# A two-layer decoder step on one core: the last additions of gathered rows partly on TensorE, and the samples' rows summed and normalized in four groups of partitions ahead of the last tile

## The chip, the core and the metric

One core of a Trainium2 chip runs the whole program. The metric is the time of one execution in device microseconds. Three runs of the kernel before gave 1462.3, 1465.44 and 1460.7 us, median 1462.3. The engines are TensorE (PE, and PEld for its weight loads), VectorE (DVE), ScalarE (ACT), GpSimd (POOL) and SyncE (SP); SP, ACT and POOL issue DMAs.

## What is computed

The reference runs a trunk of two layers over a prompt of 512 rows and over 8 sample rows, all 1024 wide. A layer is a mixer (attention and a gated recurrence in layer 0, causal mean pooling in layer 1) and then a mixture of 32 experts, of which each row uses two. The end of a layer and of the program, cut from the reference:

```python
    for layer in range(DEPTH):
        ...
        x = x + mix.astype(x.dtype)
        h = rmsnorm(x, norm_ffn[layer])
        x = x + hier_moe(h, ...)
    y = rmsnorm(x, norm_final)
```

`rmsnorm(x, g)` is `x * rsqrt(mean(x*x) + eps) * g` row by row, in float32 throughout.

## The kernel before

The 520 rows stand in SBUF as five tiles `x[:, t, :]`: tiles 0 to 3 have the prompt's 128 rows each, tile 4 (`NT`) has the 8 sample rows on 8 partitions. `TILES` is 5.

The experts of a layer are taken in 16 pairs (`PAIRS`), 64 gathered rows for each expert of a pair. SP streams three weight matrices for each pair into a ring of slots; in the first four pairs (`TURNS`) of a layer a fourth slot in the arena (`fourth`) takes part. PE computes gate products and up products (`products`), DVE and ACT make the activation, PE computes the results, and ACT scales them into `yst`. POOL gathers each pair's rows and scatters each pair's results but the last's into `y_rows` in HBM, through its own DMA queue. Each of the 520 rows has two places there, set 0 and set 1.

When the last pair has read its weights, `load_results` on SP brings `y_rows` back: one DMA for each tile into `gat[t]`, which has the two sets side by side and signals `x_in[t]`. The last pair's own results don't go through HBM. PE multiplies `memT`, a map of rows, with `yst`, in `rows_of_last(t)`, into the two PSUM banks from `LAST_BANK[t]` on, and signals `last_done`.

DVE then does, tile by tile, `combine(l, t)` (x plus set 0, and plus set 1 unless `ADDED_BY_PE[l]` lists it) and `add_last(l, t)` (x plus the two PSUM banks, signal `moe_added`). What `ADDED_BY_PE` lists is added by PE in the same PSUM group, by matmuls of the identity with the gathered rows: before the change that is set 1 of tile 3 and both sets of the samples, in layer 1 alone. For layer 0, `combine` and `add_last` feed the pooled mixer of layer 1: `pooled_rows` (DVE), `mix` (PE), `mixed_columns` (ACT), `maps` (PE), where the first `maps` waits until three tiles have had `add_last`.

At the end of the program each tile goes through ACT's `mean_root` (a Square with a sum along the row at L919, a root at L920), DVE's `normed_rows` (a reciprocal at L1270 and a product with root and gain at L1271), and a store that ACT issues at L1250. All queues are in the order of the program text. DVE's loop is `combine(u)`, `add_last(u)`, then the normalization of tile `u - 1`; ACT's loop is the root of tile `u`, then the store of tile `u - 1`. The samples are the last tile in every queue. Lines in the trace: L732 the gathers of `load_results`, L1202 and L1210 ACT's two instructions of a pair, L1570 and L1573 the sets in `combine`, L1583 `add_last`, L2202 `mix`, L1153 `mixed_columns`, L2223 `maps`, L2238 and L2252 or L2276 the products and results of experts, L2437 the transposes of the next pair's rows, L2503 the gathered sets on PE and L2504 the last pair's rows, L845 POOL's gather.

Of the kernel before, what the change touches and what calls it, by code (L numbers as in the profile page):

```python
# [75 lines left out]
def shape_constants():  # L76
# [44 lines left out]
    for g, w in enumerate(WINDOWS):  # L121
        for b in range(NB):
# [4 lines left out]
            (("c_zero", np.zeros((1, ZEROS))), ("c_onehot", onehot), ("c_square", square), ("c_small", small), ("c_masks", masks), ("c_pool", pools))}  # L127


def build(nc, a, outs, consts):  # L130
# [11 lines left out]
    with ExitStack() as ctx:  # L142
# [93 lines left out]
        ADDED_BY_PE = ((), ((NT - 1, 1), (NT, 0), (NT, 1)))  # L236
# [78 lines left out]
        ecmp = at(26900, NOV, NE)  # L315
        fourth = [at(lo, PIECE) for lo in (0, 22216)]
# [73 lines left out]
        QUERIES, LOGITS, PROBS_TURNED, ATTENDED, GATES_TURNED, HEADS_TURNED = range(1, 7)  # L390
# [3 lines left out]
        LB_EXPED, SAMPLE_ROOT, DECODE_EXPED, HEAD_ROOTS, GATES_OUT, LATE_OUT = range(1, 7)  # L394
# [236 lines left out]
        def _(sp):  # L631
# [93 lines left out]
            def load_results(l):  # L725
# [86 lines left out]
        def _(pool):  # L812
# [43 lines left out]
            for l in range(2):  # L856
# [11 lines left out]
                for i in range(PAIRS):  # L868
# [7 lines left out]
                    if l == 0 and i == TURNS - 1:  # L876
# [7 lines left out]
                        for g in range(NG):  # L884
                            pool.dma_start(poolw[:, g], a["pool_w"][0, g].rearrange("(k p) c -> p k c", p=P)).then_inc(pool_in, 16)
                pool.wait_ge(y_stored, 16 * (PAIRS - 1) * (l + 1))
# [23 lines left out]
        def _(act):  # L910
# [330 lines left out]

            for u in range(TILES + 1):
                if u < TILES:
                    act.wait_ge(moe_added, TILES + u + 1)
                    mean_root(4, u, x[0:rows_of(u), u, :], spare)
                t = u - 1
                if t >= 0:
                    act.wait_ge(y_final, t + 1)
                    dst = y_prompt.rearrange("b (t p) d -> p (b t) d", p=P)[:, t, :] if t < NT else y_sample.rearrange("b t d -> (b t) d")
                    act.dma_start(dst, x[0:rows_of(t), t, :]).then_inc(stored, 16)  # L1250

            act.wait_ge(stored, 16 * (1 + TILES))
# [8 lines left out]
        def _(dve):  # L1261
# [314 lines left out]
            def add_last(l, t):  # L1576
# [5 lines left out]
                dve.wait_ge(last_done, TILES * l + t + 1)  # L1582
# [27 lines left out]
            def experts(l):  # L1610
# [97 lines left out]
                else:  # L1708
# [154 lines left out]
            for u in range(TILES + 1):  # L1863
                if u < TILES:
                    if u < NT:
                        combine(1, u)
                    add_last(1, u)
# [718 lines left out]
```

## Time and profile before

| | us |
|---|---|
| median of the three runs | 1462.3 |
| profiled execution, whole | 1464.38 |
| its span, first to last instruction | 1462.6 |
| PE busy | 1270.1 (87%) |
| DVE busy | 358.3 (24%) |
| ACT busy | 247.4 (17%) |
| POOL busy | 83.6 (6%) |
| DMA over the span | 492.94 MB, 337 GB/s |
| mean granted TensorE clock | 0.948 |

Busy shares are means over stages with different limits. In the views of the trace times are in microseconds from the span's start. A line of the timeline gives start, duration, engine, line, operation, output and input with shapes, and a count; in brackets stands the engine's idle time before it and what ended that. A float32 matmul shows as two passes, two records each.

### The profile page before, as it was taken

How to read it: one execution, taken by the hardware profiler on the slowest of the kernel's cores; microseconds unless marked ns; L12 is line 12 of the kernel's file. 1: busy time of each engine (PE TensorE's matmuls, PEld its weight loads, DVE VectorE, ACT ScalarE, POOL GpSimd, SP SyncE). 2: the span in 40 equal slices, each digit the busy share in tenths (PEclk: the TensorE clock that was granted, in tenths of full speed). 3: DMA queues.
4: the chain of work that ended last, by engine and by line, in shares of the span. 5: the costliest groups of instructions: out<-in, count | busy, mean ns of one | idle time of the engine just before them, and what ended most of it. 6: DMA issues, size and time to landing. Idle time of an engine off the chain costs nothing.

```text
span 1462.6 us, 14567 instructions
## 1 busy us (share of the span) xinstructions
PE 1270.1 (87%) x5864; PEld 614.8 (42%) x5864; DVE 358.3 (24%) x826; ACT 247.4 (17%) x442; POOL 83.6 (6%) x101
## 2 busy tenths in 40 slices
PE   7999999999999877878878798999978777888886
PEld 3688965644543322223322235843333222232332
DVE  2065487522431000010100016551010000010006
ACT  3243643342110000000000003410000000000002
POOL 1000000000000100000000000000000000000000
PEclk9999999999999989999999999889999999999999
DMA  9435667327489999999999999369999999999995
GB/s 347 106 83 169 220 189 200 109 80 317 187 333 429 425 402 422 429 426 425 426 426 426 427 413 370 135 255 418 427 429 425 429 426 428 428 421 425 422 416 212
DMA packets 82446, 492.94 MB, mean 337 GB/s; under 512 B 17197, under 2 KB 21965, under 8 KB 59350
## 3 DMA queue, kind: packets, MB, share of 16 engines
q1 hardware_dynamic: 65968, 449.35, 75.5%
q0 software_dynamic: 13568, 37.03, 7.6%
q10 hardware_dynamic: 2862, 5.91, 1.1%
q8 instruction: 31, 0.51, 0.1%
q14 instruction: 17, 0.14, 0.0%
HBM read 479.75 MB, written 36.56 MB: 353 GB/s over the span
## 4 chain that ended last, share of the span: by engine, by line
PE 52%; DMA 37%; DVE 7%; issue 2%; ACT 2%; ACTq 0%; SPq 0%; DVEq 0%
DMA ring<-in_moe_w 35%; PE ps L2238 22%; PE ps L1912 5%; PE ps L1905 4%; PE ps L2164 3%; PE ps L2276 3%; PE ps L2350 1%; PE ps L2223 1%; PE ps L2263 1%; PE ps L2252 1%; PE ps L2304 1%; DVE arena L1366 1%; PE ps L2202 1%; PE ps L1954 1%; PE ps L2293 1%
## 5 line engine op out<-in xcount | busy, mean ns | idle before, releaser
L2238 PE MATMUL ps<-ring,arena 128*64 128x512 f32 x1920 | 470.0, 648 | 110.3 <-DMA ring<-in_moe_w 108.4
L2238 PEld LDWEIGHTS ps<-ring,arena 128*64 128x64 f32 x1920 | 146.8, 148 | 428.8 <-issue 279.4
L1781 DVE TENSOR_TENSOR arena<-arena,ps 128x512 f32<-128x512 f32 x32 | 22.0, 687 | 773.5 <-ACT arena L1202 773.5
L2276 PE MATMUL ps<-ring,arena 128*64 128x512 f32 x832 | 187.0, 602 | 26.3 <-issue 18.3
L2276 PEld LDWEIGHTS ps<-ring,arena 128*64 128x64 f32 x832 | 68.5, 138 | 126.9 <-issue 118.1
L1905 PE MATMUL ps<-arena,ring 128*128 128x260 f32 x512 | 115.7, 384 | 0.9 <-ACT arena L936 0.9
L1202 ACT ACTIVATE arena<-ps 128x512 f32<-128x512 f32 x32 | 19.1, 597 | 570.0 <-PE ps L2238 570.0
L1905 PEld LDWEIGHTS ps<-arena,ring 128*128 128x128 f32 x512 | 96.0, 190 | 17.0 <-issue 1.7
L1210 ACT ACTIVATE arena<-ps,arena 128x1024 f32<-128x1024 f32 x32 | 35.6, 1114 | 325.9 <-PE ps L2276 280.9
L1912 PE MATMUL ps<-ring,arena 128*128 128x512 f32 x192 | 86.0, 594 | 0.0
L845 POOL DMA_INDIRECT arena<-hn_rows,arena x30 | 30.6, 1021 | 528.7 <-PE ps L2437 477.0
L2164 PE MATMUL ps<-ring,arena 128*128 128x512 f32 x128 | 56.6, 595 | 0.0
L1912 PEld LDWEIGHTS ps<-ring,arena 128*128 128x128 f32 x192 | 35.3, 190 | 37.3 <-issue 36.8
L851 POOL DMA_INDIRECT y_rows<-arena x30 | 30.3, 1010 | 333.9 <-ACT arena L1210 333.9
L2437 PEld LDWEIGHTS ps<-arena 128*128 128x128 f32 x240 | 28.8, 191 | 26.5 <-issue 23.5
L1682 DVE TENSOR_TENSOR arena<-ps,arena 128x1024 f32<-128x1024 f32 x32 | 38.9, 1214 | 1.8 <-PE ps L2359 1.8
L2437 PE MATMUL ps<-arena 128*128 128x128 f32 x240 | 34.5, 287 | 2.1 <-DMA arena<-hn_rows,arena 2.1
L2462 PE MATMUL ps<-arena 128*128 128x128 f32 x128 | 23.9, 309 | 13.2 <-DVE arena L1781 13.2
L2164 PEld LDWEIGHTS ps<-ring,arena 128*128 128x128 f32 x128 | 23.7, 190 | 26.8 <-issue 26.8
L919 ACT ACTIVATE arena<-arena 128x1024 f32<-128x1024 f32 (+1 forms) x25 | 26.3, 1053 | 49.1 <-DVE arena L1608 26.9
L1786 DVE COPY arena<-ps 128x512 f32<-128x512 f32 x32 | 22.1, 692 | 32.0 <-PE ps L2462 32.0
L2238 PE MATMUL ps<-arena 128*64 128x512 f32 x128 | 28.3, 594 | 0.0
(316 smaller groups left out, 1049.1 us busy)
## 6 DMA issues: line engine op xcount, KB each, us to landing
ring<-in_moe_w SPq DMA_DIRECT2D x78, 4096.0 KB, 22.7
ring<-in_moe_w SPq DMA_DIRECT2D x40, 1024.0 KB, 12.7
arena<-in_moe_w SPq DMA_DIRECT2D x12, 2048.0 KB, 16.8
ring<-in_w_in SPq DMA_DIRECT2D x6, 2048.0 KB, 20.3
y_rows<-c_zero POOLq DMA_DIRECT2D x2, 4160.0 KB, 17.8
ring<-in_moe_w SPq DMA_DIRECT2D x4, 2048.0 KB, 20.3
ring<-y_rows SPq DMA_DIRECT2D x8, 1024.0 KB, 17.9
arena<-in_x_prompt SPq DMA_DIRECT2D x8, 512.0 KB, 6.0
```

The lines of the kernel that those rows point to most:

```text
L845: pool.indirect_dma_start(out=to, out_offset=None, in_=hn_rows[l][:, :], in_offset=bass.IndirectOffsetOnAxis(ap=slots, axis=0), bounds_che ...
L851: pool.indirect_dma_start(out=rows[:, :], out_offset=bass.IndirectOffsetOnAxis(ap=slots, axis=0), in_=of, in_offset=None, bounds_check=2 * ...
L919: link(nc.scalar.activation(junk_[0:n], x_, ACT.Square, accum_out=r_))
L1210: nc.scalar.activation(yst, ps[:, 5:7, :].rearrange("p a b -> p (a b)"), ACT.Copy, scale=scale).then_inc(y_out, 1)
L1682: V.tensor_tensor(xgT, ps[:, b:b + 2, :].rearrange("p a (k c) -> p (a k) c", k=4), wide(gain_of_rows[:, l, :], [P, KC, 2 * CAP], 2), ALU.m ...
L1905: last = T.matmul(ps[:, piece % 2, 0:HALF], w1v[:, slot, k, m * P:(m + 1) * P], hT[:, k, part * HALF:(part + 1) * HALF], start=(k == 0), s ...
L1912: last = T.matmul(ps[:, piece % 2, :], hT[:, k, m * P:(m + 1) * P], w1v[:, slot, k, :], start=(k == 0), stop=(k == KC - 1))
L2164: last = T.matmul(ps[:, b + c, :], catT[:, k, t * P:(t + 1) * P], w1v[:, WOUT_SLOT + c, k, :], start=(k == 0), stop=(k == KC - 1))
L2238: last = T.matmul(ps[r_, 2 + j, :], xgT[:, k, r_], w[:, k, :], start=(k == 0), stop=(k == KC - 1))
L2276: last = T.matmul(ps[r_, 5 + c, :], hactT[:, k, r_], w[:, k, c * 512:(c + 1) * 512], start=(k == 0), stop=(k == FC - 1))
L2437: last = T.transpose(ps[:, k // 4, (k % 4) * P:(k % 4 + 1) * P], xg[:, k:D:KC], ident)
L2462: t_ = T.transpose(ps[:, 4, k * P:(k + 1) * P], hact[:, k:FE:FC], ident)
```

## The change

At the end of layer 1 PE adds set 1 of tiles 0, 2 and 3 (tile 3's it added before); DVE keeps set 0 of all prompt tiles and set 1 of tile 1. The samples come ahead of tile 3 in the order of the gathers, of PE, and of ACT. Their 8 rows are no longer 8 partitions of 1024 columns but four groups of partitions (0 to 7, 32 to 39 and so on) with 256 columns each. PE builds them in one PSUM bank from both sets, from x and from the last pair's rows, by matmuls of 256 columns on 32 output partitions each. ACT squares that with a sum along the row; PE adds the four partial sums with the new constant `c_fold`, ahead of tile 3's own rows; ACT takes the root; DVE multiplies with root and gain from PSUM; and ACT stores four pieces. POOL loads the constant and the gain, cut in four groups, after the fourth pair of layer 1. In `rows_of_last` all gathered matmuls of a tile come first and the waits for `yst` and `memT` stand behind those of tile 0. In layer 0 only DVE's order changes, by one swap. One wait is added in the branch for overfull experts.

```diff
@@ constants and places
+            (("c_zero", ...), ("c_fold", np.tile(np.eye(32), (4, 4))), ...
+        LAST_ORDER = ((0, 1, 2, 3, NT), (0, 1, 2, NT, 3))
-        ADDED_BY_PE = ((), ((NT - 1, 1), (NT, 0), (NT, 1)))
+        ADDED_BY_PE = ((), ((0, 1), (2, 1), (3, 1), (NT, 0), (NT, 1)))
+        fold = at(22216, P)
+        gain_apart = at(22216 + P, D // 4)
+        y_apart = at(22472 + P, D // 4)
+        junk_apart = at(22728 + P, D // 4)
+        r_apart = at(22984 + P, 1)
@@ SP, load_results
-                for t in range(TILES):
+                for t in LAST_ORDER[l]:
@@ POOL, after the scatter of a pair
+                    if l == 1 and i == TURNS - 1:
+                        pool.wait_ge(y_done, PAIRS + TURNS)
+                        pool.dma_start(fold, consts["c_fold"]).then_inc(pool_in, 16)
+                        for g in range(4):
+                            pool.dma_start(gain_apart[32 * g:32 * (g + 1)],
+                                           a["norm_final"][g * D // 4:(g + 1) * D // 4]...partition_broadcast(32)...).then_inc(pool_in, 16)
@@ ACT, the end
+            def sample_root():
+                act.wait_ge(last_done, TILES + LAST_ORDER[1].index(NT) + 1)
+                nc.scalar.activation(junk_apart, ps[:, LAST_BANK[NT], 0:D // 4], ACT.Square, accum_out=r_apart).then_inc(act_step, 1)
+                act.wait_ge(sample_step, LAST_SUMMED)
+                nc.scalar.activation(r_apart, ps[:, LAST_BANK[NT] + 1, 0:1], ACT.Sqrt, bias=eps, scale=1.0 / D).then_inc(root[0], 1)
+
             for u in range(TILES + 1):
                 if u < TILES:
-                    act.wait_ge(moe_added, TILES + u + 1)
-                    mean_root(4, u, x[0:rows_of(u), u, :], spare)
+                    t = LAST_ORDER[1][u]
+                    if t == NT:
+                        sample_root()
+                    else:
+                        act.wait_ge(moe_added, TILES + min(u, NT - 1) + 1)
+                        mean_root(4, t, x[:, t, :], spare)
+                if u:
+                    t = LAST_ORDER[1][u - 1]
+                    act.wait_ge(y_final, u)
+                    if t < NT:
+                        act.dma_start(y_prompt...[:, t, :], x[:, t, :]).then_inc(stored, 16)
+                    else:
+                        for g in range(4):
+                            act.dma_start(y_sample...[:, g * D // 4:(g + 1) * D // 4],
+                                          y_apart[32 * g:32 * g + NB]).then_inc(stored, 16)
@@ DVE, between the layers
-                    for t in range(2):
-                        combine(0, t)
-                        add_last(0, t)
+                    combine(0, 0)
+                    combine(0, 1)
+                    add_last(0, 0)
+                    add_last(0, 1)
@@ DVE, the end (the loop over tiles is replaced)
+            def sample_normed():
+                dve.wait_ge(root[0], TILES * 2 + LAST_ORDER[1].index(NT) + 1)
+                link(V.reciprocal(r_apart, r_apart))
+                dve.wait_ge(pool_in, 16 * (4 + NG + 5))
+                V.scalar_tensor_tensor(y_apart, ps[:, LAST_BANK[NT], 0:D // 4], r_apart, gain_apart, ALU.mult, ALU.mult).then_inc(y_final, 1)
+
+            combine(1, 0)
+            combine(1, 1)
+            add_last(1, 0)
+            add_last(1, 1)
+            combine(1, 2)
+            combine(1, 3)
+            dve.wait_ge(router_in, 16 * 13)
+            final_rows(0)
+            add_last(1, 2)
+            final_rows(1)
+            final_rows(2)
+            add_last(1, 3)
+            sample_normed()
+            final_rows(3)
@@ PE, rows_of_last
                     if of_others:
                         pe.wait_ge(x_in[t], 16 * l + 32)
+                        for c in range(2):
+                            for k in of_others:
+                                T.matmul(... ident[0:n, 0:n], gat[t][0:n, k, c * 512:(c + 1) * 512], ...)
+                    if t == 3 and l == 1:
+                        pe.wait_ge(act_step, LAST_SQUARED)
+                        T.matmul(ps[:, LAST_BANK[NT] + 1, 0:1], fold, r_apart, start=True, stop=True).then_inc(sample_step, 1)
+                    if t == 0:
+                        pe.wait_ge(y_out, PAIRS * (l + 1))
+                        pe.wait_ge(memT_ready, 2 * l + 2)
                     for c in range(2):
...
+                def samples_of_last():
+                    pe.wait_ge(pool_in, 16 * (4 + NG + 5))
+                    pe.wait_ge(moe_added, TILES + 2)
+                    pe.wait_ge(x_in[NT], 16 * l + 32)
+                    for k in range(3):
+                        rows = x[0:NB, NT, :] if k == 2 else gat[NT][0:NB, k, :]
+                        for g in range(4):
+                            T.matmul(ps[32 * g:32 * g + 32, LAST_BANK[NT], 0:D // 4], ident[0:NB, 0:32], rows[:, g * D // 4:(g + 1) * D // 4], ...)
+                    for g in range(4):
+                        last = T.matmul(ps[32 * g:32 * g + NB, LAST_BANK[NT], 0:D // 4], memT[:, SEQ:TOK], yst[:, g * D // 4:(g + 1) * D // 4], ...)
                     last.then_inc(last_done, 1)
@@ PE, the order of the last rows
-                for t in range(TILES):
-                    rows_of_last(t)
+                for t in LAST_ORDER[l]:
+                    if l == 1 and t == NT:
+                        samples_of_last()
+                    else:
+                        rows_of_last(t)
```

## Rows read from the trace of the kernel before

**Rows 1.** Page, chain that ended last, shares of the span by engine.
```profile
PE 52%; DMA 37%; DVE 7%; issue 2%; ACT 2%; ACTq 0%; SPq 0%; DVEq 0%
```

**Rows 2.** The chain in order of time, last expert pairs: start, us, what.
```profile
1372.70 20.70 DMA ring<-in_moe_w
1393.44 9.94 PE ps L2238 x32
```

**Rows 3.** Timeline of the last 60 us, chosen lines of all engines.
```profile
1403.29 1.15 PE L2437 MATMUL ps<-arena 128*128 128x128 f32 x8
...
1436.79 1.22 DVE L1570 TENSOR_TENSOR arena<-ring,arena 128x1024 f32<-128x1024 f32 x1 [6.32 <-DMA ring<-y_rows]
1437.85 1.11 ACT L1210 ACTIVATE arena<-ps,arena 128x1024 f32<-128x1024 f32 x1 [9.63 <-PE ps L2252]
...
1439.01 5.42 PE L2504 MATMUL ps<-arena 128*128 128x512 f32 x12 [1.40 <-ACT arena L1210]
...
1441.11 1.22 DVE L1583 TENSOR_TENSOR arena<-arena,ps 128x1024 f32<-128x1024 f32 x1 [1.83 <-PE ps L2504]
...
1442.43 1.06 ACT L919 ACTIVATE arena<-arena 128x1024 f32<-128x1024 f32 x1 [1.95 <-DVE arena L1583]
...
1443.61 0.29 ACT L920 ACTIVATE arena<-arena 128x1 f32<-128x1 f32 x1
...
1448.39 1.88 PE L2503 MATMUL ps<-arena 8*8 8x512 f32 x4
...
1452.96 1.03 PE L2504 MATMUL ps<-arena 128*8 128x512 f32 x2
...
1457.25 0.14 DVE L1270 RECIPROCAL arena<-arena 128x1 f32<-128x1 f32 x1
...
1458.74 2.15 ACTq L1250 DMA_DIRECT2D out<-arena  x2
...
1459.05 1.27 DVE L1271 SCALAR_TENSOR_TENSOR arena<-arena 8x1024 f32<-8x1024 f32 x1
```

**Rows 4.** The line of ACT's last stores: durations min/median/max, first and last start.
```profile
L1250 ACTq DMA_DIRECT2D out<-arena x5: 338/338/537, 1447.4 to 1460.3; - x5
```

**Rows 5.** The gathers of tiles 0 to 2, then landing of 0 to 2, and tile 3.
```profile
L732 SPq DMA_DIRECT2D ring<-y_rows x3: 367/470/2329, 1422.7 to 1423.6; - x3
...
DMA to landing us min/median/max: 14.1/16.2/18.2
...
DMA to landing us min/median/max: 18.7/18.7/18.7
```

**Rows 6.** Timeline of four-group matmuls; then groups of 128x256 instructions out of PSUM.
```profile
301.68 3.64 PE L2072 MATMUL ps<-ring,arena 128*32 128x512 f32 x32
...
L1012 ACT ACTIVATE arena<-ps 128x256 f32<-128x256 f32 x4 | 1.5, 378 | 2.3 <-PE ps L1972 2.3
...
L1386 DVE SCALAR_TENSOR_TENSOR arena<-ps,arena 128x256 f32<-128x256 f32 x4 | 1.7, 420 | 2.1 <-PE ps L1961 2.1
```

**Rows 7.** Busy time by stretch: PE, PEld, DVE, ACT, POOL; PEclk, DMA share, GB/s.
```profile
1438.00:1440.00 2.00, 0.99 (x3) 0.51 (x4) 1.24 (x2) 1.98 (x2) 0.00 (x0) 1.00 0.51 197
1456.00:1458.00 2.00, 0.00 (x0) 0.00 (x0) 1.97 (x4) 0.94 (x2) 0.00 (x0) 0.80 0.47 193
```

**Rows 8.** Timeline at the seam of the layers, chosen lines.
```profile
887.26 8.95 PE L2504 MATMUL ps<-arena 128*128 128x512 f32 x20 [1.40 <-ACT arena L1210]
...
898.22 0.60 ACT L1153 ACTIVATE arena<-ps 128x512 f32<-128x512 f32 x1 [0.30 <-PE ps L2202]
...
899.31 3.72 PE L2223 MATMUL ps<-arena 128*128 128x256 f32 x16 [1.13 <-DVE arena L1583]
```

**Rows 9.** Stretch 1100:1150 (columns as rows 7); POOL's queue in 1100:1125: packets, MB, share.
```profile
1100.00:1150.00 50.00, 39.48 (x168) 13.55 (x166) 2.51 (x3) 2.82 (x3) 3.02 (x3) 0.93 1.01 428
...
q0 software_dynamic: 275, 0.43, 4.5%
```

**Rows 10.** DMA issues, layer 0's gather behind the fourth pair, 508:530: median us to landing.
```profile
arena<-hn_rows,arena POOLq DMA_INDIRECT x1, 39.4
```

More of the change, by code:

```diff
@@ L1861, in _, with final_rows @@
             experts(1)
[L1863 to L1867, printed above, removed]
-                t = u - 1
-                if t >= 0:
-                    if t == 0:
-                        dve.wait_ge(router_in, 16 * 13)
-                    normed_rows(4, t, t, x[0:rows_of(t), t, :], gain[0], x[0:rows_of(t), t, :]).then_inc(y_final, 1)
+            def sample_normed():
[3 more added lines that the diff above has]
+                V.scalar_tensor_tensor(y_apart, ps[:, LAST_BANK[NT], 0:D // 4], r_apart, gain_apart, ALU.mult, ALU.mult).then_inc(y_final, 1)
+            def final_rows(t):
+                normed_rows(4, LAST_ORDER[1].index(t), t, x[:, t, :], gain[0], x[:, t, :]).then_inc(y_final, 1)
+            combine(1, 0)
[12 more added lines that the diff above has]
+            final_rows(3)
         @block.tensor
@@ L2499, in rows_of_last @@
                         pe.wait_ge(x_in[t], 16 * l + 32)
+                        for c in range(2):
+                            for k in of_others:
+                                T.matmul(ps[0:n, LAST_BANK[t] + c, :], ident[0:n, 0:n], gat[t][0:n, k, c * 512:(c + 1) * 512],
+                                         start=(k == of_others[0]), stop=False)
+                    if t == 3 and l == 1:
[4 more added lines that the diff above has]
+                        pe.wait_ge(memT_ready, 2 * l + 2)
                     for c in range(2):
-                        cols = slice(c * 512, (c + 1) * 512)
-                        for k in of_others:
-                            T.matmul(ps[0:n, LAST_BANK[t] + c, :], ident[0:n, 0:n], gat[t][0:n, k, cols], start=(k == of_others[0]), stop=False)
-                        last = T.matmul(ps[0:n, LAST_BANK[t] + c, :], memT[:, t * P:t * P + n], yst[:, cols],
+                        last = T.matmul(ps[0:n, LAST_BANK[t] + c, :], memT[:, t * P:t * P + n], yst[:, c * 512:(c + 1) * 512],
                                         start=not of_others, stop=True)
+                    last.then_inc(last_done, 1)
+                def samples_of_last():
[5 more added lines that the diff above has]
+                        for g in range(4):
+                            T.matmul(ps[32 * g:32 * g + 32, LAST_BANK[NT], 0:D // 4], ident[0:NB, 0:32], rows[:, g * D // 4:(g + 1) * D // 4],
+                                     start=(k == 0), stop=False, skip_group_check=True, tile_position=(0, 32 * g))
+                    for g in range(4):
+                        last = T.matmul(ps[32 * g:32 * g + NB, LAST_BANK[NT], 0:D // 4], memT[:, SEQ:TOK], yst[:, g * D // 4:(g + 1) * D // 4],
+                                        start=False, stop=True, skip_group_check=True, tile_position=(0, 32 * g))
                     last.then_inc(last_done, 1)
```

21 lines of the change are left out of this document (9 added, 12 removed).

## The prediction

> **What bounds the kernel now.** I read the chain of waits first, by engine [rows 1]: PE holds 52% of the span, DMA 37%, DVE only 7%. In order of time [rows 2] the chain through the second layer's experts alternates: 20.7 us on a weight load, about 10 us of gate products, again and again; the last release by a load is at 1393.44. From there to the end PE, ACT and DVE hand over to each other and no load decides. So there are two regimes: a stretch bound by the load stream, where the 50 us from 1100 to 1150 show all 16 DMA engines busy (share 1.01) at 428 GB/s [rows 9], and a tail of 25 us behind the last expert pair. The change touches both, and the seam between the layers.
>
> The timeline of the tail [rows 3] shows DVE as the owner: its first residual addition starts at 1436.79, when a gather has landed; it waits 1.83 us for the first tile's matmul, and from 1441.11 on its instructions follow each other nearly without a gap until the samples' own normalization, which ends at 1460.32. The last store (issued at 1460.35 by ACT) ends the span at 1462.6. In this stretch DVE has 17 wide instructions (7 gathered additions, 5 additions of PSUM, 5 normalizations), each taking 1.2 to 1.3 us; the samples' two cost as much as a full tile's, because only columns count.
>
> **The change, part by part.**
>
> *The tail, DVE.* Four wide instructions go: set 1 of tiles 0 and 2 (PE adds tile 3's already before the change), the samples' PSUM addition, and their normalization, in whose place comes a 128x256 one of 0.42 us [rows 6]. That leaves 13 wide ones: 5 gathered additions (two of them tile 1's), 4 of PSUM, 4 normalizations. 4 times 1.25 less 0.42 is 4.6 us of DVE work. If DVE stayed the bound that would be the gain. I work out whether it does.
>
> *The tail, PE.* Each 512-column matmul of 128 rows costs two passes of about 0.43 us: 12 passes for tiles 0 to 2 in 5.42 us, the last one's flow-through of some 0.26 us in it [rows 3]. A tile's gathered set is 2 matmuls, 1.72 us, and its own rows 1.72 us. Tile 0's set (its gather issued at 1422.7 lands 14.1 us later, at 1436.8 [rows 5]) can run from 1437.65, beside ACT's copy that holds PE until 1439.01 today, and is through at 1439.4: 0.4 us of it isn't covered. Tile 0's rows are then done at 1441.3, tile 1's at 1443.0, tile 2's (one set more, its gather landed at 1441.8 by [rows 5]) at 1446.5. The samples take 16 matmuls of 256 columns in groups of 32 output partitions, 32 passes. The nearest row has 32 passes of 128x512 in such groups in 3.64 us [rows 6], so the four groups run beside each other and half the columns cost 1.8 us, in place of 5.6 us for the samples now (12 passes from 1448.39 on). Done at 1448.5; then tile 3's gathered set to 1450.2. What is not known is the time between the last expert's matmul and the first of tile 0, where PE passes a branch: today it lies inside 1.40 us of waiting [rows 3]. Bounds 0 and 1.4 us; I take 0.1, since other hand-overs take under 0.1 us, and keep 1.4 for the range.
>
> *The wait that is added.* Tile 3's own rows now stand behind a matmul that sums the samples' squares, and this stands behind ACT's Square of the samples. ACT works in order, so ahead of that Square it must pass the root of tile 2 and the store of tile 1. The schedule, with starts from the above and durations from [rows 3]: DVE adds tile 0's set at 1436.79, tile 1's two from its landing at 1439.3 [rows 5] until 1441.8, tile 0's PSUM rows 1441.8 to 1443.0, tile 1's 1443.1 to 1444.3, sets of tiles 2 and 3 to 1446.5, the normalization of tile 0 (0.15 + 1.28, with the hand-overs 1.4) to 1447.9, tile 2's PSUM rows until 1449.16. From the end of such an addition (1442.33) to the end of the root on ACT (1443.90) are 1.57 us [rows 3]: 1450.73. It issues tile 1's store (0.34 us [rows 4]) and squares the samples from 1451.15 (a 128x256 ACT instruction out of PSUM takes 0.38 us [rows 6], and the read of the sum ends 0.12 us behind a Square): 1451.7. PE has been idle since 1450.2. Now come the sum over the groups, two short passes (0.2 us), and tile 3's rows; from the end of ACT's instruction to DVE's start this took 1441.11 - 1438.96 = 2.15 us for tile 0 [rows 3]. So DVE starts tile 3's addition at 1454.1, though it was free at 1452.3. The queue behind PE's wait holds just that tile, but everything that is left needs it: addition to 1455.3, root on ACT (1.6 us) to 1456.9, normalization to 1458.4. The samples' own normalization (0.6 us) and root are hidden in ACT's root of tile 3.
>
> *The stores.* The last one is now tile 3's 512 KB instead of 32 KB. The 32 KB store took 1462.6 - 1460.35 = 2.25 us to the end; 480 KB more at 428 GB/s are 1.1 us, so 3.3 us. Ahead of it ACT issues four stores of the samples, from 1456.9. The issue of a store held ACT between 0.338 and 0.537 us, the longest being the 8-row one [rows 4]. Four take 1.4 to 2.1 us, through at 1458.3 to 1459.1, so up to 0.7 us of them sticks out behind DVE's end. The span would end at 1461.7 to 1462.4: 0.9 to 0.2 us less than 1462.6. I take 0.4 us less. With PE's unknown at 1.4 us, all behind moves by 1.7: 1.5 us more.
>
> *The two gathers that change places.* Samples' 64 KB ahead of tile 3's: 0.15 us at the stream's rate. Tile 3's gather landed at 1425.95 + 18.7 = 1444.65 [rows 5] and is needed at 1445.4, so nothing; were it 1 us late, 0.3 us.
>
> *The seam of the layers.* In layer 0 only DVE's order changes: the two sets of tile 1 stand ahead of tile 0's PSUM addition. This fills the idle time before it and brings the third PSUM addition, on which the first pooled map waits 1.13 us [rows 8], about 1.9 us forward by my count of DVE's instructions. But what is late next is close: PE's last-rows matmuls run from 887.26 for 8.95 us, the pooling matmuls follow, and their copy on ACT ends at 898.82, against the map's start at 899.31 [rows 8]. Gain 0.44 us, and PE passes it on, as it works nearly without a gap from there. Bounds: 0 and 0.44 us.
>
> *The new loads in the stream.* POOL issues five DMAs (64 KB of constants in pieces of 512 B, four of 32 KB in pieces of 1 KB) after the fourth pair of layer 1, in the stretch that the loads bound; each pushes the stream back by its bytes. 192 KB at 428 GB/s are 0.46 us. By time on the engines: POOL's queue had 275 packets in 4.5% of 16 engines over 25 us [rows 9], 18 us or 65 ns a packet of 1.6 KB; 256 packets at that price are 1.04 us over 16 engines. I take 0.6. On POOL's own queue the next gather stands behind them. In layer 0, with 3.33 MB ahead, that gather landed in 39.4 us [rows 10]; 192 KB are a seventeenth, 2.3 us more, and it is wanted some 30 us later. Nothing. The branch's added wait lies on a path that isn't taken.
>
> By the Trainium skill ("TensorEngine Tiling (Array Packing)", Key Properties) a change of tiling mode drains TensorE, and the samples add two changes. Here a 64-column group ends at 1403.38 [rows 2] and the 128-column one after it has started at 1403.29 [rows 3], so the trace shows no gap. Two drains of a flow-through each, 0.26 us, would move PE's 1450.2 to 1450.7, still ahead of ACT's 1451.7, and the sum would stay.
>
> **Sum.** -0.4 (tail) - 0.44 (seam) + 0.6 (loads) = -0.24 us. The profiled execution took 1464.38 us (span 1462.6 and 1.8 around it), giving 1464.1; it stands 2.1 us above the median of the three runs, 1462.3. So I forecast 1462.1 us. The bounds give -0.9 - 0.44 + 0.46 = -0.9 us to +1.5 + 0 + 1.04 = +2.5 us: 1461.4 to 1464.8.
>
> **Rivals.** (a) DVE stays the bound: the Square comes in time. Speaks for it: DVE is back to back today. Against: ACT's order, worked out above. Then tile 3's addition starts at 1452.3 and all behind it, the stores' issues too, 1.8 us sooner: 1460.3; with the low bounds (-0.9 - 1.8 - 0.44 + 0.46 from 1462.3) 1459.6. (b) Slower: PE's idle gap ahead of the last tile costs it the clock. At 1438 to 1440, behind a gap of 1.40 us, the granted clock was 1.00, the 2.4 GHz level; at 1456 to 1458, behind the last matmul's end at 1454, it was 0.80 [rows 7]. My gap is 1.5 us, near the first. If it decides, four passes cost twice 0.43 us: +1.7 us, 1463.8. It decides only if the clock falls before tile 3's rows begin at 1451.9. (c) The packed groups don't run beside each other with 8 rows: 32 passes at 0.21 us are 6.8 us, the samples end at 1453.5, the Square follows, and all is 2.4 us later: 1464.5. Against it: [rows 6]. (d) The loads hit harder than their bytes, the gather among them late, or a gain beyond the count: a difference over 0.3%.
>
> **How the numbers follow.** A measurement can tell about 0.3%, 4.4 us. Chances: forecast 0.68, (a) 0.12, (b) 0.07, (c) 0.05, (d) 0.08, of it slower 0.05 and faster 0.03. Only (d) leaves the 0.3%: faster 0.03, same 0.92, slower 0.05. The range takes in the bounds and (a) to (c), and a few tenths for the median of three runs: 1459.4 to 1465.2.
>
> **What would show it.** Right: a PE group of gathered matmuls ahead of ACT's last copy has ended; DVE waiting near 2 us for tile 3's rows; PE idle 1 to 2 us, released by ACT's 128x256 Square; the samples' 32 passes in about 2 us; first map of layer 1 half a microsecond earlier; last load's release later by about 0.2 us. Wrong: DVE without a gap up to tile 3's addition; the granted clock under 1.00 in the tail while PE works; the samples over 4 us; a pair of layer 1 waiting for its gather.

## The result, and the profile after

The changed kernel took 1458.42 us, the median of 19 runs (1454.09 to 1464.18); 19 runs of the kernel before, on the same chip beside them, had a median of 1464.07 us (1459.83 to 1467.41). The ratio is 0.9957, with a 95% interval of 0.9944 to 0.9971: 6.3 us less (4.2 to 8.2); the difference of the two medians is 5.7 us. I had forecast 0.24 us less and a time of 1462.1 us, with 0.9 us less at the far end of the counted part, and the median lies below my range of 1459.4 to 1465.2 us. The forecast's rival (d) had a chance of 0.03 for a gain over 0.3%, but no mechanism for it.

The chain that ended last, by engine, in the page of the changed kernel (for [rows 1]):

```profile
PE 50%; DMA 39%; DVE 6%; issue 2%; ACT 2%; SPq 0%; ACTq 0%; DVEq 0%; POOLq 0%
```

PE has lost two points, but these shares point at nothing here: two points are 29 us, far more than the whole gain, and over the profiles below PE's share runs from 50 to 55% without following the time (50% in a span of 1464.5 us, 52% in one of 1452.9). I cut both profiled executions at four instructions that both have, and took the lengths between: the start of ACT's last copy of results in layer 0; the first gate product of layer 1; the start of the last gate or up product ahead of which PE waited over 3 us for a load; ACT's last copy of results in layer 1; the end of the span. Worked out from the timelines, in us:

| | start to ACT's last copy, layer 0 | seam | stream | close | tail | span |
|---|---|---|---|---|---|---|
| before | 886.09 | 82.53 | 424.82 | 44.41 | 24.75 | 1462.6 |
| changed | 885.29 | 75.54 | 425.77 | 44.46 | 23.24 | 1454.3 |
| difference | -0.80 | -6.99 | +0.95 | +0.05 | -1.51 | -8.3 |

Of 8.3 us (this pair of executions is 2 us further apart than the ratio says) 7.0 come from the seam between the layers, where the change swaps two steps of DVE, and 1.5 from the tail, which is what the change is about; how far a stage differs from one execution to the next is in the experiments. The first stretch isn't touched by the change; its 0.8 us is the spread of one execution to the next.

The seam in the timeline of the changed kernel (for [rows 8]):

```profile
886.46 8.95 PE L2554 MATMUL ps<-arena 128*128 128x512 f32 x20 [1.40 <-ACT arena L1223]
...
896.53 0.60 ACT L1166 ACTIVATE arena<-ps 128x512 f32<-128x512 f32 x1 [4.78 <-PE ps L2245]
...
897.28 3.69 PE L2266 MATMUL ps<-arena 128*128 128x256 f32 x16
...
897.43 0.60 ACT L1166 ACTIVATE arena<-ps 128x512 f32<-128x512 f32 x1 [0.29 <-PE ps L2245]
```

The last rows' matmuls take 8.95 us as before. But the first map (L2266) starts at 897.28, ahead of ACT's second copy: it needs the first copy alone, and the sum over the second half comes later. Behind the start of the last rows it is 10.82 us, before it was 12.05: 1.23 us gained, and 1.35 us by the second map (behind ACT's last copy of results it starts at 19.26 in place of 20.61 us). That is three times my 0.44.

The other 5.6 us are PE's clock: 3.8 of them up to the third tile's maps, 1.8 behind. Over the whole seam the mean granted clock was 0.88 before and 0.96 after. Busy time by stretch, first before, then changed (columns as in rows 7; PEclk is the third from the end):

```profile
910.00:915.00 5.00, 3.89 (x31) 3.55 (x30) 2.25 (x6) 1.24 (x2) 0.00 (x0) 0.95 0.97 413
915.00:920.00 5.00, 5.00 (x25) 5.00 (x25) 2.45 (x17) 0.60 (x1) 0.00 (x0) 0.50 0.87 365
920.00:925.00 5.00, 5.00 (x20) 4.53 (x20) 1.45 (x2) 3.97 (x8) 0.00 (x0) 0.53 0.00 0
```

```profile
910.00:915.00 5.00, 4.76 (x42) 4.76 (x43) 2.37 (x16) 0.79 (x2) 0.00 (x0) 1.00 1.01 428
915.00:920.00 5.00, 5.00 (x32) 4.38 (x31) 2.08 (x6) 4.13 (x9) 0.00 (x0) 1.00 0.51 216
920.00:925.00 5.00, 5.00 (x45) 4.90 (x44) 3.77 (x19) 1.68 (x3) 0.60 (x1) 1.00 0.26 105
```

In the kernel before the granted clock fell to 0.50, the level of 1.2 GHz, as the third tile's pooling began, and stayed there for 10 us (0.95, 0.50 and 0.53 over 5 us each are 0.5, 5 and 4.7 us at the low level). In the changed kernel it stays at 1.00, 2.4 GHz. What PE did ahead of the fall is plain in the kernel before:

```profile
910.24 1.04 PE L2293 MATMUL ps<-arena 128*128 128x128 f32 x8
912.38 1.98 PE L2304 MATMUL ps<-arena 128*128 128x36 f32 x16 [1.11 <-ACT arena L1135]
914.19 0.52 PE L2202 MATMUL ps<-arena 128*128 128x128 f32 x2
914.50 0.46 PE L2204 MATMUL ps<-arena 128*128 128x16 f32 x2
914.80 0.78 PE L2202 MATMUL ps<-arena 128*128 128x128 f32 x2
```

Transposes, an idle gap of 1.11 us for ACT's copy, the first router logits (36 columns a pass), and then matmuls that suddenly take 0.78 us where a moment ago they took 0.47. The changed kernel has the same sequence with the same 1.11 us of waiting, and keeps the clock.

The tail of the changed kernel, chosen lines (for [rows 3]):

```profile
1430.75 1.98 PE L2545 MATMUL ps<-ring,arena 128*128 128x512 f32 x4
1431.06 1.11 ACT L1223 ACTIVATE arena<-ps,arena 128x1024 f32<-128x1024 f32 x1 [11.33 <-PE ps L2295]
...
1432.57 3.60 PE L2554 MATMUL ps<-arena 128*128 128x512 f32 x8
1432.62 1.23 DVE L1598 TENSOR_TENSOR arena<-ring,arena 128x1024 f32<-128x1024 f32 x1 [1.51 <-DMA ring<-y_rows]
...
1439.53 1.50 PE L2566 MATMUL ps<-arena 8*32 8x256 f32 x24
...
1440.96 0.62 PE L2569 MATMUL ps<-arena 128*8 128x256 f32 x8
...
1441.51 1.98 PE L2545 MATMUL ps<-ring,arena 128*128 128x512 f32 x4
...
1444.10 0.38 ACT L1258 ACTIVATE arena<-ps 128x256 f32<-128x256 f32 x1 [0.30 <-issue]
...
1444.63 0.38 PE L2549 MATMUL ps<-arena 128*128 128x1 f32 x2 [1.14 <-ACT arena L1258]
...
1446.95 1.22 DVE L1611 TENSOR_TENSOR arena<-arena,ps 128x1024 f32<-128x1024 f32 x1 [1.62 <-PE ps L2554]
...
1449.39 1.56 ACTq L1277 DMA_DIRECT2D out<-arena  x4
...
1451.23 0.36 ACTq L1274 DMA_DIRECT2D out<-arena  x1
```

Here the forecast can be laid on the trace, landing of tile 1's gather on landing (1439.34 on 1432.62, a shift of 6.72). Tile 0's set runs beside ACT's copy, and DVE idles for tile 3's rows, 1.62 us, with PE's idle 1.14 us released by ACT's Square, as worked out. The samples take 1.98 us on PE. Tile 3's addition starts 14.33 us behind the landing (forecast 14.76), the last store is issued at 18.61 (forecast 19.0 to 19.8), and the span ends 3.07 us later (forecast 3.3).

### The profile page after: what moved, and what is told of

Its sections match the earlier page's. It is cut to its first block, busy times and chain, and to the rows that moved or that the text cites. A ratio compares the mean times of both kernels' runs of the same rounds, so it can differ in the third digit from the quotient of the medians.

```text
span 1454.3 us, 14633 instructions
## 1 busy us (share of the span) xinstructions
PE 1260.1 (87%) x5894; PEld 611.4 (42%) x5894; DVE 354.2 (24%) x823; ACT 246.7 (17%) x442; POOL 86.2 (6%) x106
## 4 chain that ended last, share of the span: by engine, by line
PE 50%; DMA 39%; DVE 6%; issue 2%; ACT 2%; SPq 0%; ACTq 0%; DVEq 0%; POOLq 0%
DMA ring<-in_moe_w 36%; PE ps L2281 19%; PE ps L1955 5%; PE ps L2319 4%; PE ps L1948 4%; PE ps L2207 3%; DMA ring<-y_rows 1%; PE ps L2266 1%; PE ps L2306 1%; PE ps L2393 1%; PE ps L2347 1%; DVE arena L1394 1%; PE ps L2554 1%; PE ps L1997 1%; PE ps L2245 1%
## 5 line engine op out<-in xcount | busy, mean ns | idle before, releaser
L2281 PE MATMUL ps<-ring,arena 128*64 128x512 f32 x1920 | 460.4, 636 | 115.5 <-DMA ring<-in_moe_w 113.6
L2281 PEld LDWEIGHTS ps<-ring,arena 128*64 128x64 f32 x1920 | 144.5, 146 | 426.7 <-issue 270.2
L2319 PE MATMUL ps<-ring,arena 128*64 128x512 f32 x832 | 188.6, 606 | 24.8 <-DMA ring<-in_moe_w 13.2
L2281 PE MATMUL ps<-arena 128*64 128x512 f32 x128 | 28.3, 594 | 0.0
```

Source lines behind the costliest of these rows:

```text
L2281: last = T.matmul(ps[r_, 2 + j, :], xgT[:, k, r_], w[:, k, :], start=(k == 0), stop=(k == KC - 1))
L2319: last = T.matmul(ps[r_, 5 + c, :], hactT[:, k, r_], w[:, k, c * 512:(c + 1) * 512], start=(k == 0), stop=(k == FC - 1))
```

## The experiments

Three theories stood after the result. S: the seam brings it, by its direct gain and by the clock. D: the swap brings its direct 1.3 us and the clock's fall is chance. T: the tail brings it. Ratios below are to runs of the kernel before beside them on the same chip; stage lengths are cut as in the table above. "Maps 3" is the start of the third tile's maps, counted from ACT's last copy of layer 0; it tells whether the clock fell in the pooling ahead of it.

**The swap alone, in the kernel before.**

```diff
-                    for t in range(2):
-                        combine(0, t)
-                        add_last(0, t)
+                    combine(0, 0)
+                    combine(0, 1)
+                    add_last(0, 0)
+                    add_last(0, 1)
```

> The kernel before with nothing but the swap between the layers (both sets of tile 1 ahead of tile 0's PSUM addition). Theory S (the seam brings most of the gain: the first map starts 1.3 us earlier, and PE, without its idle 1.13 us ahead of it, keeps the 2.4 GHz clock where the kernel before fell to 1.2 from 914 to 922): 4 to 6 us less than the kernel before, granted clock 1.00 from the first map to the third tile's pooling. Theory D (the swap is worth its direct 1.3 us and the clock falls here or not by chance): 1 to 2 us less. Theory T (the tail brings the gain): under 0.5 us less.

1460.4 us against 1465.24 (12 and 35 runs), ratio 0.9969 (0.9949 to 0.9988): 4.5 us less (1.8 to 7.5), most of the change's gain out of four lines. The seam is 75.57 us.

**The changed kernel without the swap.** The edit above, undone.

> The changed kernel with the swap between the layers undone. Theory S: 0 to 1.5 us less than the kernel before (tail -1.5, loads +0.8), and the first map is again behind an idle gap of PE near 1.1 us with the clock at 0.5 some 15 us later. Theory D: 4 to 5 us less than the kernel before on the median. Theory T: 4 to 6 us less.

1464.0 against 1465.24 us, ratio 1.0002 (0.9984 to 1.002). The medians are 1.2 us apart, the ratio says 0.3 us more: the whole of the tail and the new loads comes to nothing that can be told. Its seam is 82.56 us, as before to 0.03 us. With the run above this settles where the gain is: T falls. Its tail also shows rival (b) of the prediction for once:

```profile
1454.15 0.38 PE L2548 MATMUL ps<-arena 128*128 128x1 f32 x2 [1.77 <-ACT arena L1258]
1454.40 2.64 PE L2553 MATMUL ps<-arena 128*128 128x512 f32 x4
...
1457.14 1.22 DVE L1611 TENSOR_TENSOR arena<-arena,ps 128x1024 f32<-128x1024 f32 x1 [2.30 <-PE ps L2553]
```

Behind an idle gap of 1.77 us tile 3's rows took 2.64 us in place of 1.96, and DVE waited 2.30 us in place of 1.62. The tail of this execution was 24.90 us.

**A filling matmul in the first idle gap** (in the kernel before, ahead of the first map's wait).

```diff
                 else:
+                    T.matmul(ps[64:P, 6, :], memT[:, 0:64], yst[:, 0:512], start=True, stop=True)
                     pe.wait_ge(moe_added, 3)
```

> The kernel before with one more matmul (128 rows, 64 by 512) ahead of the wait of the first map, written to partitions of a PSUM bank that nobody reads, so that PE has work in its idle 1.13 us; the order of DVE is untouched. Theory S, clock part: no fall of the clock at 914 to 922, 3 to 5 us less than before, though the first map starts no earlier. Theory D: within 0.5 us of before.

1465.49 against 1465.24 us, ratio 0.9998 (0.9976 to 1.0021). Maps 3 at 36.47 us, seam 82.58: the fall is there to the tenth of a microsecond. The clock part of theory S, as I had put it (the idle 1.13 us ahead of the first map costs the clock), is wrong.

**The new loads alone.**

```diff
+                    if l == 1 and i == TURNS - 1:
+                        pool.wait_ge(y_done, PAIRS + TURNS)
+                        pool.dma_start(fold, consts["c_fold"]).then_inc(pool_in, 16)
+                        for g in range(4):
+                            pool.dma_start(gain_apart[32 * g:32 * (g + 1)], ...).then_inc(pool_in, 16)
```

> The kernel before with the five new DMAs alone (the constant and the gain in four groups, after the fourth pair of layer 1; nothing reads them). By the profile of the changed kernel the stretch bound by the loads became 0.77 us longer: 0.5 to 1.0 us more than before. Rival: the loads cost nothing that can be seen, under 0.3 us, and the 0.77 us is the stream's own spread.

1466.64 against 1465.24 us, ratio 1.0016 (1.0 to 1.0033), so 0 to 4.8 us more. The stream stage doesn't single them out: 424.62 us here. Over all profiles with the loads (7) it is 425.1 us on average, without (13) 424.5, and the groups spread from 423.2 to 426.7 and from 423.0 to 425.4: +0.7 us with a standard error of 0.5. That agrees with my 0.6 and isn't shown.

**A filling matmul in the second idle gap**, the 1.11 us ahead of the first router logits, in the kernel before.

```diff
+                    for _ in range(1 if l == 1 and p == 0 else 0):
+                        T.matmul(ps[:, 0, :], ident, x[:, 0, 0:512], start=True, stop=True)
                     pe.wait_ge(htile_ready, g + 1)
```

> The kernel before with one more matmul (128x128 by 512) into a free PSUM bank in PE's other idle gap at the seam, 1.11 us ahead of the first router logits of layer 1, where it waits for ACT's copy. The clock falls right behind this gap in every profile of the old order. Theory I (this idle gap, just ahead of the fall, is what costs the clock): no fall in the pooling of the third tile, 4 to 5 us less than before. Theory P (what decides is when the stretch of short matmuls starts, not whether PE idles in it): the fall stays, within 0.5 us of before.

Maps 3 came at 32.59 us in place of 36.42, the seam was 79.42 us. Of its second profile these are the lines at the gap and the stretches behind it:

```profile
908.24 1.02 PE L2301 MATMUL ps<-arena 128*128 128x512 f32 x2
909.51 1.98 PE L2306 MATMUL ps<-arena 128*128 128x36 f32 x16 [0.25 <-ACT arena L1135]
911.32 0.47 PE L2202 MATMUL ps<-arena 128*128 128x128 f32 x2
```

```profile
909.00:914.00 5.00, 4.75 (x41) 4.49 (x41) 2.13 (x15) 1.06 (x2) 0.00 (x0) 1.00 1.04 441
914.00:919.00 5.00, 5.00 (x34) 4.64 (x33) 2.31 (x8) 3.85 (x8) 0.00 (x0) 1.00 0.49 206
```

The gap is 0.25 us, the pooling takes 0.47 us a pair again, the clock is 1.00. So work that nobody needs, put there, shortens the seam by 3.1 us; theory I had 4 to 5 us. In the whole time the first twelve runs gave only 0.9994 (0.9977 to 1.0012), which left it open; more below.

**The swap, with all behind the first map pushed late by busy work**: one and two of the first filling matmuls in the kernel with the swap.

```diff
                 else:
+                    for _ in range(1):      # range(2) in the second kernel
+                        T.matmul(ps[64:P, 6, :], memT[:, 0:64], yst[:, 0:512], start=True, stop=True)
                     pe.wait_ge(moe_added, 3)
```

> The kernel with the swap alone, and ahead of the first map one more matmul (0.86 us) that writes where nobody reads: all behind it starts 0.9 us later, without an idle gap, which gives back 0.9 of the 1.3 us that the swap brings directly. Theory P: somewhere between the swap's 1.3 us and none the fall of the clock comes back; here it may go either way: 3.5 to 4.5 us less than before if the clock stays, 0 to 1 us if it falls. Theory I (PE busy, clock kept): 3.5 to 4.5 us less.

> The same with two such matmuls, 1.7 us: all behind the first map starts 0.4 us later than in the kernel before, with PE busy throughout. Theory P: the clock falls in the third tile's pooling as before, 0 to 1 us more than before. Theory I: the clock stays at 1.00, 3 to 4 us less.

With one the first map starts 1.05 us later than with the swap alone, the clock falls, but for 7 us only, maps 3 come at 35.29 us, the seam is 80.52 us, ratio 0.9983 (0.9963 to 1.0004), between the two outcomes that theory P allowed. With two it starts 1.90 us later (0.66 later than in the kernel before); the fall is back in full, maps 3 at 36.76, seam 82.86 us, ratio 1.0014 (0.9997 to 1.0031). PE worked without a pause from the last rows to the transposes there:

```profile
895.60 2.05 PE L2203 MATMUL ps<-arena 128*128 128x128 f32 x16
897.58 1.93 PE L2220 MATMUL ps<-arena 128*64 128x512 f32 x4
899.44 3.72 PE L2226 MATMUL ps<-arena 128*128 128x256 f32 x16
```

```profile
914.00:923.00 9.00, 9.00 (x44) 8.91 (x44) 3.16 (x20) 2.79 (x6) 0.00 (x0) 0.51 0.61 256
```

So, by one profile of each kernel so far, the fall hangs on two things: on when the stretch of short passes begins (a microsecond of delay brings it back), and on what PE does in the idle gap in that stretch (filled, the fall is gone though nothing starts earlier). The filling matmul closes the gap and adds 0.86 us of wide work at once; which of the two counts isn't told apart. Neither theory I nor P alone would do.

**Does it repeat?** The kernel before, unchanged, twice more; the swap alone twice more; the second filler twice more; the changed kernel once more.

> The kernel before, unchanged, for a second profile of it. Theories I and P: the granted clock falls to 0.5 about 28 us behind ACT's last copy of layer 0, in the pooling matmuls of the third tile, as in the first profile. Theory D (chance): it is as likely to be at 1.00 there.

> The kernel before, unchanged, a third profile. If the old order costs the clock each time (theory P+I), the first product of layer 1 comes 82.5 us behind ACT's last copy of layer 0 and the third tile's maps 36.4 us behind it; if it is chance, one of the two profiles here may show 32 to 33 us.

> The swap alone, a second profile. If the order decides, the third tile's maps come at 31.2 us and the first product at 75 to 77 us, the clock at 1.00 between; one profile of a kernel with the swap (the one with fillers at the end of the seam) had them at 34.2 and 79.7, so that may come too.

> The swap alone, a third profile, with the same expectations as for the second one.

> The old order with the filling matmul ahead of the first router logits, a second profile. If the filler is what kept the clock, the third tile's maps come at 32.6 us again and the first product near 79.4 us; if its first profile was luck, at 36.4 and 82.5 us.

> The old order with the filling matmul, a third profile and more times. With the clock kept in the third tile's pooling the first product comes 3 to 6 us earlier than in the kernel before, and the whole time should follow by 2 to 5 us; the first twelve times showed only 0.9 us (interval -3.4 to +1.8).

> The changed kernel unchanged, for a second profile. The seam's length (75.5 us), the clock's course in it and the tail (23.2 us) should repeat within 0.3 us; if the tail is 24 us or more, the clock falls in it now and then, as in the profile of the kernel without the swap, where tile 3's last rows took 2.64 us.

| order of DVE, filler | maps 3, us | seam, us |
|---|---|---|
| old (before, three profiles) | 36.42, 36.46, 36.45 | 82.53, 82.56, 82.55 |
| old, with loads; with the tail; with the first filler | 36.21, 36.81, 36.47 | 81.10, 82.56, 82.58 |
| old, second filler (three profiles) | 32.59, 32.58, 32.58 | 79.42, 76.44, 79.41 |
| swap alone (three profiles) | 31.23, 31.24, 31.23 | 75.57, 76.65, 76.66 |
| changed kernel (two profiles) | 31.24, 31.28 | 75.54, 76.54 |

Theory D falls: six of six profiles of the old order have the clock's fall ahead of the third maps, the five of the table with the swap don't, and three of three with the second filler don't. (One further kernel with the swap does, below.) The ten more times of the filler gave 0.9971 (0.9957 to 0.9985), 4.2 us less; weighted together with the first twelve's 0.9994 I estimate 0.9980 (0.9969 to 0.9991), 2.9 us less, so its gain is also in the clock on the wall.

The second profile of the changed kernel missed two of its expectations. The seam was 76.54 us and not 75.5, and the tail was 24.35 us without a fall of the clock while PE worked: tile 3's rows took 1.96 us, as in the first profile. There ACT's last copy came 1.2 us earlier (the close was 43.21 us in place of 44.46) and the gathers did not. Nor is the seam of one kernel one number: the second filler has 79.42, 76.44 and 79.41 us, the swap alone 75.57, 76.65 and 76.66, with falls further back in the seam that come, stay away or last longer.

**Swap and second filler together.**

> The swap alone, with the filling matmul ahead of layer 1's first router logits as well. Both kernels then have the clock at 1.00 through the third tile's pooling, so this one against the filled one of the old order (first product 79.4 us behind ACT's last copy of layer 0) shows the swap's direct worth. Theory I+P: the seam is 1.4 us shorter up to the third tile's maps, the first product comes at 75 to 78 us. Rival: the filling matmul's 0.86 us of work delays a chain that is now without slack there, and the seam is longer than with the swap alone (75.6 us).

Maps 3 at 31.23 us, as with the swap alone, and 1.35 us ahead of the filler alone: with the clock kept in both, this is the swap's direct worth. The seam is 76.50 us, ratio 0.9954 (0.9934 to 0.9975).

**Fillers at the end of the changed kernel's seam**, one ahead of the last ranks and one ahead of the first product.

```diff
+                for _ in range(l):
+                    T.matmul(ps[:, 6, :], ident, x[:, 0, 0:512], start=True, stop=True)
                 ranks(TILES - 1)
...
                 slot_sums(4)
+                for _ in range(l):
+                    T.matmul(ps[:, 2, :], ident, x[:, 0, 0:512], start=True, stop=True)
```

> The changed kernel with two more matmuls that nobody reads at the end of layer 1's seam: one ahead of the last tile's ranks, where PE idles 0.7 us, one ahead of the first product, where it idles 0.8 us. In the changed kernel the granted clock is 0.5 from 958 to 963 and the first 64 products take 16.0 us in place of 13.9. Theory I (idle gaps among short matmuls cost the clock): the fall goes, the first pair's gate and up products take 13.9 us, 1 to 2 us less than the changed kernel. Rival: fall stays or moves, the fillers cost their time: 0 to 1 us more.

The first pair's products take 13.95 us in place of 16.03, with no fall there:

```profile
968.47 13.95 PE L2281 MATMUL ps<-ring,arena 128*64 128x512 f32 x64
```

But this execution had a fall in the third tile's pooling in spite of the swap (maps 3 at 34.22, seam 79.72 us), ahead of both fillers, so they can't be its cause. It is the one of nine profiles with the swap and no delay that has it:

```profile
912.00:917.00 5.00, 3.89 (x35) 3.65 (x33) 2.16 (x9) 1.02 (x1) 0.00 (x0) 0.97 1.02 437
917.00:922.00 5.00, 5.00 (x25) 5.00 (x26) 1.87 (x13) 1.17 (x3) 0.00 (x0) 0.50 0.76 318
922.00:927.00 5.00, 5.00 (x26) 4.52 (x24) 1.54 (x3) 4.63 (x9) 0.00 (x0) 0.85 0.01 3
```

The traces say a little more. By the granted clock in stretches of 1 us, the fall begins 28.3 to 28.7 us behind ACT's last copy of layer 0 in seven of the nine profiles that have it, and 28.0 us behind it in two, this one and the changed kernel without the swap. So the moment of the fall doesn't follow the work: the third tile's pooling starts at 28.1 us in the old order and at 26.75 us with the swap. That fits the other eight with the swap: all their work stands 1.3 us further ahead of such a moment. Here the moment itself came 0.3 to 0.7 us sooner than in the seven, which takes part of that back. It is argued from these starts, not shown by a run. Since the clock's course ahead of the last products differs too, their 13.95 us can't be put down to the fillers.

The ratio is 0.9956 (0.9936 to 0.9975), the changed kernel's own: nothing gained that can be told.

**ACT's Square of the samples ahead of the root of tile 2**, in the changed kernel.

```diff
+                        if t == 2:
+                            sample_squared()     # the wait for last_done and the Square, taken out of sample_root
                         act.wait_ge(moe_added, TILES + min(u, NT - 1) + 1)
```

> The changed kernel, with ACT's Square of the samples moved ahead of the root of tile 2 (its own root stays where it was). Theory A (ACT's order makes tile 3's rows late): DVE's wait of 1.6 us for them falls under 0.4 us, the tail from ACT's last copy to the end is 1.2 to 1.5 us shorter than the changed kernel's 23.24, PE's idle 1.14 us is gone. Rival: the gathers or PE's matmuls are late next and the tail gains under 0.5 us. In the whole time: 0.5 to 2 us less than the changed kernel, 5.5 to 8 us less than before.

```profile
1438.76 1.22 DVE L1603 TENSOR_TENSOR arena<-ring,arena 128x1024 f32<-128x1024 f32 x1 [2.13 <-DMA ring<-y_rows]
...
1447.62 0.38 ACT L1258 ACTIVATE arena<-ps 128x256 f32<-128x256 f32 x1 [2.31 <-DVE arena L1304]
...
1448.65 0.28 PE L2554 MATMUL ps<-arena 128*128 128x1 f32 x2
1448.79 1.96 PE L2559 MATMUL ps<-arena 128*128 128x512 f32 x4
...
1451.24 1.21 DVE L1616 TENSOR_TENSOR arena<-arena,ps 128x1024 f32<-128x1024 f32 x1
```

PE no longer idles ahead of the sum, and DVE's wait for tile 3's rows is gone (the line of 1451.24 has no idle time). From the landing of tile 1's gather to the end are 19.84 us, against 21.68, 21.56 and 21.55 in the three profiles of the changed kernel's own order without a fall in the tail: 1.8 us. The stage from ACT's last copy didn't show it (23.23 against 23.24), since that gather landed 2.13 us behind DVE's need here and 1.51 us there. The whole time: 1457.05 against 1465.76 us, ratio 0.9946 (0.9929 to 0.9964), the lowest of all; against the changed kernel's 0.9957 the intervals overlap, so in the whole time its 1.8 us aren't told apart.

**Early Square and second filler together.**

> The changed kernel with the early Square of the samples and with the filling matmul ahead of layer 1's first router logits. If the filler guards the clock in the third tile's pooling, the third tile's maps come at 31.2 us behind ACT's last copy of layer 0; the early Square takes 1 us off the tail. Expected: 7 to 10 us less than the kernel before, within 2 us of the kernel with the early Square alone; more than 2 us slower than that one would mean that the filler costs more than it guards.

Ratio 0.9949 (0.9931 to 0.9967); seam 76.66, tail 22.37 us, 19.77 us from the landing to the end. The filler adds nothing to the swap, which keeps the clock without it.

## Why the prediction was wrong

*The step that failed is the seam, "Gain 0.44 us, and PE passes it on".* It stood in the sum with 0.44 us, and the seam became 6.0 and 7.0 us shorter in the two profiles of the changed kernel. It was mis-sized twice. First, the direct gain: I took the end of ACT's second copy (898.82) as what is late next. The first map's matmuls need only the first half of the columns; with DVE early they begin right behind the pooling matmuls. The gain is 1.35 us (maps 3 at 32.58 and at 31.23 us, clock kept in both). The code says so (the wait for the second half stands behind `g % 2 == 0`), and I read the wait of the second copy's line instead. (DVE's third addition came 1.5 us forward, not the 1.9 that I had counted; it no longer decides.)

Second, and worth more, "PE passes it on" took durations as fixed. The kernel before spends 10 us on end at 1.2 GHz there, and its seam has a mean granted clock of 0.88; I had looked at the granted clock at the tail alone and wrote a rival on the clock for the tail alone. The direct 1.35 us also moved the short-pass stretch out of the fall: maps 3 came 5.2 us earlier in all, the first product 6 to 7 us. This was in the trace of before (PEclk 0.50 at 915 to 920), though how far a shift would remove it was not; it is a cause that should have had a rival, a price (the third tile's pooling takes 6.58 us at the low clock and 3.57 at the high one) and a place in the range.

*The tail, term by term.* DVE's work, PE's pace, the four groups side by side, the uncovered 0.4 us, DVE's wait behind ACT's order: each as forecast, within 0.4 us. The end came 21.6 us behind tile 1's landing in place of 22.4 to 23.1: the four stores' issues took 1.56 us together (the first held ACT 0.537 us, the other three 0.298 to 0.317, below my low bound of 0.34 for each), the last store 3.07 us and not 3.3, PE's branch nothing that shows. In these profiles the tail is 1.5 us shorter, not 0.4: close and tail together are 69.16, 69.13 and 69.30 us in the kernel before and 67.70 and 67.60 in the changed one. Over all profiles it is less. The fourteen with the old tail have 67.8 to 69.5 us, on average 68.8; the four with the changed tail and ACT's own order have 67.3 to 69.3, on average 68.0: 0.9 us less, with a standard error of 0.5.

```profile
L1277 ACTq DMA_DIRECT2D out<-arena x4: 298/317/537, 1449.4 to 1450.6; - x4
```

*Rival (a)* didn't happen, and the early Square shows its price: 1.8 us, as worked out. *Rival (b)* happens in some executions: one profile of six with the changed tail, 0.7 us on PE and not 1.7, since only the later passes ran at the low clock. *Rival (c)* fell: 32 passes in 1.98 us with 8 rows in each. By the Trainium skill ("TensorEngine Tiling (Array Packing)", Key Properties) each change of tiling mode drains the array; the three groups follow each other at 1439.53, 1440.96 and 1441.51 with each start ahead of the modelled end of the one before, so no drain shows here either.

*The loads* are neither confirmed nor refuted (+0.7 +- 0.5 us in the stream stage).

*The gathers.* DVE's wait for tile 1's was 1.26 or 1.27 us in three of the six profiles with the changed tail, the 1.3 that the forecast's schedule has, and 1.51, 2.09 and 2.13 us in the others, up to 0.8 us more. In the changed order this is on the path, and was a term I had taken as fixed.

Sum of what was measured: seam -6.0 to -7.0, tail -0.9 (-1.5 in the first pair), loads +0.7 (not clear of noise), which is -6.2 to -7.2, against -6.3 us by the ratio (4.2 to 8.2 less).

What stays open: why the clock falls at that point, and what sets the moment. It was moved in both directions (a delay of 1 to 2 us brings it back, a filled gap removes it), but one profile with the swap had it all the same, and no rule is drawn from it here. The first filler, as much work 12 us earlier, did nothing.

## What to carry to other kernels

A small edit on a path that other work hides can be worth more than its own microseconds if PE's granted clock is low just behind it: read the clock in 5 us stretches along every stage that the change shifts, and price each stretch of 0.50 as a rival. Where PE must wait among short matmuls, a matmul that nobody reads can be cheaper than the wait (0.9 us of work for 3 us), but only where the clock would fall otherwise: of the places tried, one gained, and with the swap in place the same filler added nothing. And cut two profiles into stages at instructions that both have before explaining a difference of medians; the stage with the gain was not the one that the change was about. Take more than one profile of each kernel for it: the tail's 1.5 us of the first pair were 0.9 over all, and the seam of one unchanged kernel came out up to 3 us apart.

## What the runs showed of the hardware

The course of the granted clock can repeat closely from one execution to the next: three profiles of the kernel before have the third maps at 36.42 to 36.46 us and the seam at 82.53 to 82.56, though the whole spans run from 1461.7 to 1466.4 us. It need not: three profiles of the second filler have the third maps at 32.58 and 32.59 us and the seam at 79.42, 76.44 and 79.41. The stream stage runs from 422.95 to 426.71 us over all profiles.

In the kernel before the granted clock fell to 0.50 at 914.5 us and stayed there to 924.7, though PE had not been idle for more than 1.13 us at a time since the first pooling at 896.1. Just ahead of the fall it had transposes, a gap of 1.11 us and passes of 36 columns.

The first 8-row store held ACT 0.537 us, with 1024 columns (before) as with 256 (after); the three of 256 columns right behind it held it 0.298, 0.317 and 0.317 us. Stores of 128 rows by 1024 columns held it 0.338 to 0.372 us. So the issue of a store of 8 KB costs nearly as much of ACT's time as that of one of 512 KB.

Four column groups of 32 partitions ran beside each other with 8 rows in each: 24 passes of 256 columns took 1.50 us.
